# Two transformer blocks: the first head's first eight experts chosen from both lists' best eight, and four rows summed ahead of the sixth query block

## The reference, cut to what matters

```python
q = jnp.einsum('bsd,dq->bsq', h, w_pq).reshape(b, s, PEER_HEADS, 2, PEER_HALF)
sub_scores = jnp.einsum('bshpc,pnc->bshpn', q, subkeys).astype(jnp.float32)
top_s, top_i = lax.top_k(sub_scores, PEER_TOPK)
cand_s = (top_s[..., 0, :, None] + top_s[..., 1, None, :]).reshape(b, s, PEER_HEADS, n_cand)
cand_i = (top_i[..., 0, :, None] * PEER_NKEYS + top_i[..., 1, None, :]).reshape(b, s, PEER_HEADS, n_cand)
fin_s, fin_pos = lax.top_k(cand_s, PEER_TOPK)
expert_idx = jnp.take_along_axis(cand_i, fin_pos, axis=-1)
gates = jax.nn.softmax(fin_s, axis=-1).astype(h.dtype)
# per chunk of 128 tokens, with the 8 x 16 experts of each token:
act = jax.nn.gelu(jnp.einsum('chkd,cd->chk', jnp.take(u, ec, axis=0), hc), approximate=False) * gc
out = jnp.einsum('chk,chkd->cd', act, jnp.take(v, ec, axis=0))
```

## Time and profile before

| | us |
|---|---|
| median of 3 runs (1414.19 to 1417.28) | 1416.06 |
| the profiled execution, whole | 1414.91 |
| its span, first to last instruction | 1413.0 |
| PE busy in the span | 1301.2 (92%) |
| DVE busy | 946.2 (67%) |
| ACT busy | 499.9 (35%) |
| POOL busy | 464.3 (33%) |

### The profile page before, as it was taken

How to read it: one execution, slowest core, us unless ns; L and a number is a source line. 1 busy time by engine, 2 the same in 40 slices (tenths; PEclk the granted TensorE clock), 3 DMA queues, 4 the chain that set the end, 5 groups by cost and what they waited for, 6 DMA issues and landing times.

```text
span 1413.0 us, 25002 instructions
## 1 busy us (share of the span) xinstructions
PE 1301.2 (92%) x9620; PEld 1233.6 (87%) x9620; DVE 946.2 (67%) x2091; ACT 499.9 (35%) x975; POOL 464.3 (33%) x326
## 2 busy tenths in 40 slices
PE   9999999999999997886888797988899999999998
PEld 8999999998989997886878787888886789989997
DVE  4688987666577777859585767855525647666665
ACT  5533456355222222212102221211225446553443
POOL 1588831100144564553536354555203000000000
PEclk9999999999999998999989998999999999999999
DMA  7555554552799999999999999999862033355552
GB/s 283 194 187 188 186 183 150 185 182 83 268 426 426 409 425 427 427 427 428 427 426 426 426 427 427 427 428 427 334 283 90 31 114 127 136 207 179 180 191 77
DMA packets 58907, 398.29 MB, mean 282 GB/s; under 512 B 6464, under 2 KB 9536, under 8 KB 11328
## 3 DMA queue, kind: packets, MB, share of 16 engines
q0 software_dynamic: 36864, 268.45, 45.1%
q1 hardware_dynamic: 21952, 128.61, 25.4%
HBM read 395.99 MB, written 1.05 MB: 281 GB/s over the span
## 4 chain that ended last, share of the span: by engine, by line
PE 60%; DMA 18%; DVE 11%; issue 7%; ACT 3%; POOL 1%; DVEq 0%; POOLq 0%; ACTq 0%
DMA rows_late<-peer_uv_dram,stage 17%; PE bank L777 11%; PE bank L778 11%; PE bank L779 11%; PE bank L1054 10%; PE bank L741 6%; PE bank L761 4%; DVE rows_late L2174 3%; ACT w_hi L1278 1%; POOL rows_late L677 1%; PE bank L901 1%; PE bank L925 1%; DVE w_lo L553 1%; PE bank L1129 1%; PE bank L1010 1%
## 5 line engine op out<-in xcount | busy, mean ns | idle before, releaser
L1054 PE MATMUL bank<-diag,rows_late 128*128 128x128 f32 x2816 | 330.6, 281 | 24.5 <-ACT diag L1475 24.5
L1054 PEld LDWEIGHTS bank<-diag,rows_late 128*128 128x128 f32 x2816 | 327.4, 197 | 26.8 <-ACT diag L1475 26.8
L2174 DVE SCALAR_TENSOR_TENSOR rows_late<-rows_late,squares 128x1024 f32<-128x1024 f32 x176 | 213.3, 1227 | 112.8 <-DMA rows_late<-peer_uv_dram,stage 103.0
L677 POOL DMA_INDIRECT rows_late<-peer_uv_dram,stage x165 | 197.6, 1198 | 134.1 <-PE bank L1054 82.7
L1054 PE MATMUL bank<-diag,rows_early 128*128 128x128 f32 x1280 | 167.3, 296 | 67.2 <-ACT diag L1475 67.1
L1054 PEld LDWEIGHTS bank<-diag,rows_early 128*128 128x128 f32 x1280 | 161.9, 210 | 72.4 <-ACT diag L1475 72.1
L1278 ACT ACTIVATE w_hi<-raw 128x2048 fp32r<-128x2048 f32 x94 | 179.3, 1909 | 117.4 <-PE bank L779 109.9
L777 PE MATMUL bank<-x_hi_a,w_hi 128*128 128x256 f32 x672 | 190.9, 284 | 2.7 <-DVE x_lo_a L1708 1.8
L778 PE MATMUL bank<-x_lo_a,w_hi 128*128 128x256 f32 x672 | 190.1, 283 | 0.0
L779 PE MATMUL bank<-x_hi_a,w_lo 128*128 128x256 f32 x672 | 190.1, 283 | 0.0
L553 DVE TENSOR_TENSOR w_lo<-raw,w_hi 128x2048 fp32r<-128x2048 f32 x66 | 151.2, 2292 | 48.6 <-ACT w_hi L1278 43.8
(11 more groups left out here) (387 smaller groups left out, 1873.8 us busy)
## 6 DMA issues: line engine op xcount, KB each, us to landing
raw<-w_in_dram SPq DMA_DIRECT2D x28, 1024.0 KB, 4.9
raw<-w_up_dram SPq DMA_DIRECT2D x16, 1024.0 KB, 4.9
raw<-w_down_dram SPq DMA_DIRECT2D x16, 1024.0 KB, 4.8
rows_late<-w_in_dram SPq DMA_DIRECT2D x10, 1024.0 KB, 9.0
raw<-w_kv_dram SPq DMA_DIRECT2D x8, 1024.0 KB, 4.8
raw<-sc_w_out_dram SPq DMA_DIRECT2D x4, 1024.0 KB, 4.8
raw<-cf_w_pw_dram SPq DMA_DIRECT2D x4, 1024.0 KB, 4.8
raw<-w_mix_out_dram SPq DMA_DIRECT2D x4, 1024.0 KB, 5.0
```

What stands on the lines that cost most here:

```text
L677: g.indirect_dma_start(out=expert_rows(k), out_offset=None, in_=T["peer_uv"], in_offset=bass.IndirectOffsetOnAxis(ap=stage_at[:, k:k + 1], ...
L1054: mm = nc.tensor.matmul(ct(Y_ACC[c][t // 4], t % 4, P), expert_rows(k)[:, D + t * P:D + (t + 1) * P], ct(diag, k % DIAGS, P), start=first ...
L2174: w_.scalar_tensor_tensor(out=row, in0=row, scalar=1.0, in1=h_tok[:, c * D:(c + 1) * D], op0=ALU.mult, op1=ALU.mult, accum_out=pre[:, side ...
```

## The change

Five things change; the work is otherwise the same.

1. VectorE's choice for head 0: the first eight experts come from the 64 sums of the best eight of each list, with a look-up over 8 in place of 16. Only then are the second eight of each list found and all 256 sums made; the eight that were taken are masked by their positions (a pass of 256 elements for each), and the second eight found among the rest.
2. TensorE sums the rows 0 to 3 of head 0 ahead of queries(5), and the other twelve behind it.
3. ScalarE makes the first four diagonals of head 0 ahead of the drains of queries(4) and of the scores (1, 0).
4. In head 0's products the weights come ahead of the piece of choice, where both are due.
5. GpSimd issues the first four gathers of head 1 ahead of head 0's last (row 13), which waits for queries(5).

```diff
@@ gpsimd: order of the gathers @@
             late_query = ROWS_EARLY + LATE_PLACES.index(QUERY_HOMES[RING])
-            after_queries = ROWS_EARLY + LATE_PLACES.index(QUERY_HOMES[-1]) + 1
-            gathers(0, expert, [*range(8, late_query), *range(after_queries, TOPK), *range(late_query, after_queries)], first=True)
+            last_query = ROWS_EARLY + LATE_PLACES.index(QUERY_HOMES[-1])
+            gathers(0, expert, [*range(8, late_query), *range(last_query + 1, TOPK), *range(late_query, last_query)], first=True)
             pool.wait_ge(experts_known, 1)
             stage_head(1, stages[1])
-            gathers(1, stages[1])
+            gathers(1, stages[1], range(GROUP))
+            gathers(0, expert, [last_query], first=True)
+            gathers(1, stages[1], range(GROUP, TOPK))
@@ tensor @@
             pair_scores(1, 0)
-            queries(PH - 3)
...
-            add_rows(0, 0, first=True)
+            add_rows(0, 0, range(GROUP), first=True)
+            queries(PH - 3)
+            add_rows(0, 0, range(GROUP, TOPK))
             queries(PH - 2)
@@ scalar @@
             exp_gates(0)
-            drain_queries(4)
-            drain_scores(1, 0)
             s.activation(sink_e[:, 0:1], eps[:, 0:1], ACT.Gelu)
...
             head(0, 0, which=slice(0, 1))
+            drain_queries(4)
+            drain_scores(1, 0)
             drain_queries(PH - 3)
             head(0, 0, which=slice(1, 4))
@@ vector: first_head_experts goes, choose_first_head comes (its helpers cut) @@
+            def choose_first_head():
...
+                dve.wait_ge(first_score_out, 1)
+                on_both(lambda x, w, v8, i8: w_.max(out=v8[:, 0:8], in_=x))
+                on_both(lambda x, w, v8, i8: w_.max_index(out=i8[:, 0:8], in_max=v8[:, 0:8], in_values=x))
+                w_.tensor_copy(idx[:, :, 0:8], of_list[:, :, 0:8]).then_inc(dve_step, 1)
...
+                sums(best_sums, 8)
+                link(w_.max(out=ov[:, 0:8], in_=best_sums))
+                link(w_.max_index(out=oi[:, 0:8], in_max=ov[:, 0:8], in_values=best_sums))
+                look_up(0, 3)
+
+                on_both(lambda x, w, v8, i8: w_.match_replace(out=w, in_to_replace=v8[:, 0:8], in_values=x, imm_value=LOWEST))
+                on_both(lambda x, w, v8, i8: w_.max(out=v8[:, 8:16], in_=w))
+                on_both(lambda x, w, v8, i8: w_.max_index(out=i8[:, 8:16], in_max=v8[:, 8:16], in_values=w))
+                link(w_.tensor_copy(idx[:, :, 8:16], of_list[:, :, 8:16]))
+                sums(all_sums, TOPK)
+                link(w_.scalar_tensor_tensor(out=position.rearrange("p (a b) -> p a b", a=TOPK),
...
+                link(w_.tensor_scalar(taken, position, place[:, 0:1], None, ALU.is_equal))
+                for k in range(1, 8):
+                    link(w_.scalar_tensor_tensor(out=taken, in0=position, scalar=place[:, k:k + 1], in1=taken,
+                                                 op0=ALU.is_equal, op1=ALU.add))
+                link(w_.scalar_tensor_tensor(out=all_sums, in0=taken, scalar=LOWEST, in1=all_sums, op0=ALU.mult, op1=ALU.add))
+                link(w_.max(out=ov[:, 8:16], in_=all_sums))
+                link(w_.max_index(out=oi[:, 8:16], in_max=ov[:, 8:16], in_values=all_sums))
+                look_up(8, 4)
...
-            choose_head(0)
+            choose_first_head()
             choose_head(1)
@@ vector: products @@
+                    due = k >= GROUP and k % GROUP == 1 and k != choose_at
+                    if due and weigh_first:
+                        weigh(k // GROUP - 1, k // GROUP * GROUP - GROUP, k // GROUP * GROUP)
                     if k >= 3 and k % 2:
                         next(pieces, None)
-                    if k >= GROUP and k % GROUP == 1 and k != choose_at:
+                    if due and not weigh_first:
                         weigh(k // GROUP - 1, k // GROUP * GROUP - GROUP, k // GROUP * GROUP)
...
-            products(0, 0, 0, choose_next(0))
+            products(0, 0, 0, choose_next(0), weigh_first=True)
```

More of the change, by code:

```diff
@@ L1989, in chain @@
                 return step, made
-            def first_head_experts(idx):
-                x, w, ov, oi = ct(cand, 0), top_work[0][:], ct(fin_v, 0, TOPK), ct(fin_i, 0, TOPK)
+            def choose_first_head():
+                lists = [(ct(scores, a, NKEYS), top_work[a][:, 0:NKEYS], ct(top_v, a, TOPK), ct(top_i, a, TOPK)) for a in range(2)]
+                ov, oi = ct(fin_v, 0, TOPK), ct(fin_i, 0, TOPK)
+                all_sums, best_sums = ct(cand, 0), ct(cand, 1)[:, 0:64]
+                position, taken, place = pos_row[:], root_buf[:], gel[:, 0:8]
+                vals = top_v[:, 0:K2].rearrange("p (a k) -> p a k", k=TOPK)
+                of_list = top_i[:, 0:K2].rearrange("p (a k) -> p a k", k=TOPK)
+                idx = top_f[:, 0:K2].rearrange("p (a k) -> p a k", k=TOPK)
                 part_of = part_i[:].rearrange("p (a k) -> p a k", a=2)
@@ L1996, in first_head_experts, with on_both @@
                 picked = pick[:].rearrange("p (a k) -> p a k", a=2)
-                def half(lo):
-                    ks, four = slice(lo, lo + 8), [P, 2, 8, TOPK]
-                    w_.tensor_single_scalar(part_of[:, 0, ks], oi[:, ks], 4, op=ALU.logical_shift_right)
-                    link(w_.tensor_single_scalar(part_of[:, 1, ks], oi[:, ks], TOPK - 1, op=ALU.bitwise_and))
+                iota = k_of("iota")
+                square = [P, TOPK, TOPK]
+                def on_both(call):
+                    for a in range(2):
+                        tok = done(call(*lists[a]), dve_step)
+                    dve.wait_ge(*tok)
@@ new lines, in sums, with look_up @@
+                def sums(out, n):
+                    link(w_.tensor_tensor(out.rearrange("p (a b) -> p a b", a=n),
+                                          vals[:, 0, 0:n].unsqueeze(2).to_broadcast([P, n, n]),
+                                          vals[:, 1, 0:n].unsqueeze(1).to_broadcast([P, n, n]), ALU.add))
+                def look_up(lo, bits):
+                    n = 1 << bits
+                    ks, four = slice(lo, lo + 8), [P, 2, 8, n]
+                    w_.tensor_single_scalar(part_of[:, 0, ks], oi[:, ks], bits, op=ALU.logical_shift_right)
+                    link(w_.tensor_single_scalar(part_of[:, 1, ks], oi[:, ks], n - 1, op=ALU.bitwise_and))
@@ L2008, in half @@
+                    link(w_.tensor_tensor(eq, eq, idx[:, :, 0:n].unsqueeze(2).to_broadcast(four), ALU.mult))
                     link(w_.tensor_reduce(picked[:, :, ks], eq, AX, ALU.add))
-                    link(w_.scalar_tensor_tensor(out=number_of[:, 0, ks], in0=picked[:, 0, ks], scalar=float(NKEYS),
+                    link(w_.scalar_tensor_tensor(out=picked[:, 0, ks], in0=picked[:, 0, ks], scalar=float(NKEYS),
                                                  in1=picked[:, 1, ks], op0=ALU.mult, op1=ALU.add))
-                    w_.tensor_copy(expert[:, ks], number_of[:, 0, ks]).then_inc(first_known, 1)
@@ L2013, in first_head_experts @@
-                link(w_.max(out=ov[:, 0:8], in_=x))
-                link(w_.max_index(out=oi[:, 0:8], in_max=ov[:, 0:8], in_values=x))
-                half(0)
-                link(w_.match_replace(out=w, in_to_replace=ov[:, 0:8], in_values=x, imm_value=LOWEST))
-                link(w_.max(out=ov[:, 8:16], in_=w))
-                link(w_.max_index(out=oi[:, 8:16], in_max=ov[:, 8:16], in_values=w))
-                half(8)
+                    w_.tensor_copy(expert[:, ks], picked[:, 0, ks]).then_inc(first_known, 1)
@@ new lines, in choose_first_head @@
+                link(w_.scalar_tensor_tensor(out=place, in0=number_of[:, 0, 0:8], scalar=float(TOPK),
+                                             in1=number_of[:, 1, 0:8], op0=ALU.mult, op1=ALU.add))
+                link(w_.tensor_scalar(taken, position, place[:, 0:1], None, ALU.is_equal))
+                for k in range(1, 8):
+                    link(w_.scalar_tensor_tensor(out=taken, in0=position, scalar=place[:, k:k + 1], in1=taken,
+                                                 op0=ALU.is_equal, op1=ALU.add))
```

18 lines of the change are left out of this document (7 added, 11 removed).

## The result

The changed kernel takes 1419.75 us (median of 9 runs, 1418.17 to 1422.87); the kernel before, run on the same chip beside it, 1414.90 us (9 runs, 1412.43 to 1417.94). The ratio is 1.0035, with a 95% interval of 1.0025 to 1.0044: slower by 4.85 us. The forecast was 1.35 us slower than its base, the first median of 1416.06, and its range ended at 1419.7, which is 3.6 us above that base. So the time lies just outside the range, and the difference, with both kernels run side by side, 1.2 us outside.

What follows compares the result with a forecast made beforehand. Gathered-row DMA bounds the stage, with TensorE deciding at row 33. TensorE 1.04 + 1.73 = 2.77 us late makes row 33 1.35 us later: span 1413.0 + 1.35 = 1414.35, or 1417.4 us against the median; range 1414.0 to 1419.7.

Steps and rivals of the forecast that it cites:

- The first gather: GpSimd's first gather of head 0, at the stream's start: issued at 375.73, 2.44 us sooner.
- The second eight: VectorE's later choice for head 0: last cast at about 386.0, 4.66 us later, hidden by 4 us.
- weights(1): VectorE's weights for head 0's second four rows: at 419.8, after a wait for the Gelu, against 421.22 before.
- weights(2): VectorE's weights for head 0's rows from row 8: at 432.15, 1.04 us later, as piece 3 replaces piece 5.
- the wait ahead of row 8: TensorE's wait in head 0: grows from 2.48 to 4.9 us by the order of the pieces.
- the early start would be lost: The stream begins 2.44 us sooner but runs dry before head 2's first gather, issued at 460.38.
- the thin spell ahead of head 2: Low DMA rates around head 2's first gather: 287 and 238 GB/s behind 459, called the stream's weak point.
- The slower rival: No slack at row 33 and a deeper clock fall: stream 2.8 to 3.6 us late, 1418.9 to 1419.7; chance 0.14.
- What that wait does to the clock: TensorE behind the wait ahead of row 8: half clock adds 1.73 us, making head 1's rows 2.77 us late.
- The upper end of the clock term: Largest lateness allowed for TensorE at head 1's rows with the clock fallen: 3.6 us in all.
- What the stream makes of it: Head 2's first gather at 460.38, 5.6 us from issue to use: row 33 used at 466.0, 1.35 us later.
- from there all is as before, moved: Everything behind row 33, to the stage's end, only shifts; head 3's first gather has a full queue ahead.

Runs made afterwards that it cites:

- the choice alone: New choice for head 0 only, all orders on TensorE, ScalarE, GpSimd and the weights as in the kernel before; ratio 1.0000 to the kernel before.
- The filled wait: Changed kernel with 20 unused matmuls of zeros in TensorE's wait ahead of row 8; ratio 0.9994 to the kernel before.
- the kernel with 18 products: Kernel before with 18 unused matmuls of zeros ahead of head 1's rows, nothing else altered; 1418.38 us against 1415.00, ratio 1.0024.
- the pure delays: Kernel before with 5, 13 or 18 unused matmuls of zeros ahead of head 1's rows; ratios 1.0000, 1.0006 and 1.0024.
- the choice with weights first: New choice, old orders, but head 0's weights(1) and weights(2) ahead of their pieces of choice; ratio 0.9998 to the kernel before.
- the same kernel with 13 products ahead of head 1's rows: Kernel before with 13 unused matmuls of zeros ahead of head 1's rows; ratio 1.0006.
- the kernel before with the weights first: Kernel before with only head 0's weights(1) and weights(2) put ahead of their pieces of choice; ratio 0.9998.

## Why the prediction missed

**Right.** The first gather: 2.44 us sooner forecast, 2.44 measured. The second eight: cast at 386.0 forecast, 386.21 with the start taken off; the seven masked passes took 3.61 us, against 7 x 0.51. Rows 0 to 3 at 404.85 (404.83 measured), queries(5) behind them, weights(1) at 419.8 (419.60), row 4 at 420.45 (420.25), weights(2) at 432.15 (432.01), the wait ahead of row 8 4.9 us (4.99), half clock behind it. That the early start would be lost was right too, as the choice alone shows, though more than half of it went in head 1's gathers already and only 0.7 us in the thin spell ahead of head 2. The forecast's mechanism was the one at work; what failed is the size of two of its terms, and one that it put at nothing. The slower rival, "no slack at row 33", forecast the stream 2.8 to 3.6 us late, and it was 3.30 at the last row; its condition held only in part, as row 33's own time was 6.32 us and not 7.0.

**Step that failed, in size: "What that wait does to the clock".** "So I add 1.73 us" came from the nearest wait in length, 4.75 us. Measured: 2.90. The upper end of the clock term was 2.6, and of TensorE's lateness 3.6 in all; it was 3.79 at head 1's rows. The filled wait shows the term by itself. Eight waits of over 3 us with a fall and two shorter ones without made it look like a matter of length. It isn't one: in the kernel before the clock fell behind a wait of 2.30 us too (the eight rows from 539.44 took 16.19 us), and in the changed kernel it held behind 3.37 us (the eight rows from 860.86 took 14.56).

**Step that failed, in size: "What the stream makes of it".** The prediction took the time from issue to use of head 2's first gather as 5.6 us, the middle of 4.3 and 7.0, and let all behind it follow row 33; so 1.42 us of TensorE's lateness of 2.77 were to vanish. Issue to use was 6.32 us (461.82 to 468.14), and in the kernel with 18 products 5.94, where the DMA moved 55 GB/s in 460 to 464. "DMA: Bandwidth & Descriptors" of the Trainium skill (section on the anatomy of one DMA on the GpSimd path) gives 4.4 us by its fit, an estimate for 1 MB; here a row behind an almost empty queue took 1.5 to 1.9 us more, with the next gather issued some 2 us behind it, and the measurement decides. The term was forecast at +1.35 and is +3.30 at the last row. Of the 1.95 us between them, 1.02 are the gather's later issue (the clock), 0.72 the longer time from issue to use, and 0.22 came behind row 33. The slack itself, measured by the pure delays at the last row, is 0.2 to 1.0 us.

**Term put at nothing: the end of the stage.** The prediction had "from there all is as before, moved". In the profiles the end took 0.92 us more: the clock fell in the last head in both, and with the new choice the late row stands ahead of the last head's row 4.

With the clock and the end put right and no slack, the sum is 1.04 + 2.90 = 3.94 us at head 2's gather (3.79 measured), 3.3 at the last row, and 4.2 with the end. The medians differ by 4.85; the remaining 0.6 us aren't placed. The upper end of the range left out the size that the clock took together with the lack of slack.

**Open.** The 0.65 us that the stream of the changed kernel gives back between row 35 and the last row, which is within the spread of that stretch; why two kernels of the same path differ by 1 to 2 us between profile and median; why the clock falls behind one wait and holds behind another of the same length.

## What to carry to other kernels

Where the transfers are the bound, count the items that must pass before the next gate opens. A stream that is started earlier but runs into the same gate only moves its idle time, and a gate that opens earlier gives nothing if the stream hasn't got there: here only both together moved the last row. What a later gate costs is worth testing with a few idle products before anything is reordered, and such a pure delay also measures the slack, which one row's time from issue to use did not. Code that is added at the beginning can shift a late row at the end. And when a reordering lengthens a wait of TensorE, add what the clock takes behind it as a range up to and past the largest fall that the profile shows (2.6 us here, against 2.90 measured), or put useful work into the wait.

## What the runs showed of the hardware

- The price of a wait for TensorE isn't ordered by its length. Rows 8 to 15 took 17.46 us behind a wait of 4.99, 16.32 behind 5.44, 16.11 behind 6.55 (14.56 at the whole clock).
- Shorter waits fall in one case and hold in another: 2.82 held in the kernel before, 3.01 held in the choice with weights first, 2.87 fell in the choice alone (row 4 took 3.52 us in place of 2.05). In the last head a wait of 2.40 fell in the kernel before and held in the same kernel with 13 products ahead of head 1's rows.
- 13 products of 128 x 128 in fp32 take 3.07 us and 18 take 4.18: some 0.23 us each at the whole clock, a ruler for delays.
- The last rows wait for one DMA engine that is behind the others. At the end of the changed kernel's stream, ahead of the last row's product at 1022.41, the DMA moves 26 GB/s for 3.5 us, a sixteenth of the 427 of the full stream, and such a tail stands in all fourteen profiles. So the mean rate of the 16 engines can show a closed hole (the kernel before with the weights first) that the rows hardly feel. That its missing 1 us went this way fits, but isn't shown.

```profile
1018.50:1022.00 3.50, 3.50 (x34) 3.50 (x33) 1.82 (x6) 1.14 (x4) 0.00 (x0) 1.00 0.06 26
```
